# Order of the condition weights in the transfer queue of a two-block transformer kernel

## What is computed

```python
def first_block(x, p, ...):                      # 256 tokens, width 1024
    h = x
    for i in range(2):
        hn = rms_norm(h, g[0])
        y = mla_mixer(hn, ...) if i == 0 else dilated_mixer(hn, ...)
        h = h + rms_norm(y, g[1])                               # closing product w_o inside the mixer
        h = h + rms_norm(swiglu(rms_norm(h, g[2]), ffn_w_in[i], ffn_w_out[i]), g[3])
        h = h + (p[i] @ ple_w_proj[i]) * sigmoid(h @ ple_w_gate[i])
    return h

def second_block(x, c, ctx, c_ctx, w_ada, b_ada, ...):
    for l in range(2):
        sh1, sc1, gt1, sh2, sc2, gt2 = split(silu(c) @ w_ada[l] + b_ada[l], 6)      # w_ada[l]: 1024 x 6144
        csh1, csc1, ...              = split(silu(c_ctx) @ w_ada[l] + b_ada[l], 6)
        xn = modulate(rms_norm_2(h, ...), sh1, sc1); xc = modulate(rms_norm_2(hc, ...), csh1, csc1)
        ...   # attention, gating, neighbourhood attention with the bias na_rpb[l], then the experts
```

## Time and profile before

| what | us |
|---|---|
| median of 3 runs | 3183.58 |
| lowest, highest | 3181.65, 3187.3 |
| the profiled execution | 3185.1 |
| its span in the profile | 3183.4 |
| TensorE busy | 2817.2 (88%) |
| GpSimd busy | 1044.3 (33%) |

### The profile page before, as it was taken

How to read it: one execution, slowest core, us unless ns; L and a number is a source line. 1 busy time by engine, 2 the same in 40 slices (tenths; PEclk the granted TensorE clock), 3 DMA queues, 4 the chain that set the end, 5 groups by cost and what they waited for, 6 DMA issues and landing times. The chain is left out here.

```text
span 3183.4 us, 33959 instructions
## 1 busy us (share of the span) xinstructions
PE 2817.2 (88%) x13329; PEld 1876.5 (59%) x13329; DVE 1311.8 (41%) x2392; ACT 930.7 (29%) x1303; POOL 1044.3 (33%) x431
## 2 busy tenths in 40 slices
PE   7999959999998798799987999998597897999885
PEld 4777638887776486577875444443485775433331
DVE  5552123334523426763345333322527545332223
ACT  0433313335333313441212222222324332222211
POOL 0277528742875244043420000000363671000000
PEclk9999979999999899999988999999799998999998
DMA  5755675555556432222233999999242456999996
GB/s 179 265 181 177 246 280 177 181 169 179 182 186 237 161 103 81 81 92 75 100 119 142 383 421 422 422 422 402 106 137 75 146 206 273 411 422 422 422 422 266
DMA packets 208913, 746.03 MB, mean 234 GB/s; under 512 B 13877, under 2 KB 15075, under 8 KB 158833
## 3 DMA queue, kind: packets, MB, share of 16 engines
q1 hardware_dynamic: 189872, 669.61, 55.5%
q0 software_dynamic: 18880, 74.22, 6.8%
HBM read 721.00 MB, written 44.27 MB: 240 GB/s over the span
## 5 line engine op out<-in xcount | busy, mean ns | idle before, releaser
L1886 POOL TENSOR_TENSOR weight_ring_r<-weight_ring,weights_high_r 128x2048 fp32r<-128x2048 f32 x136 | 622.7, 4589 | 460.2 <-ACT weights_high_r L1495 370.0
L1495 ACT ACTIVATE weights_high_r<-weight_ring 128x2048 fp32r<-128x2048 f32 x136 | 257.1, 1901 | 654.2 <-PE banks L848 415.4
L843 PE MATMUL banks<-weights_high_r,x_transposed_r 128*128 128x512 f32 x1008 | 400.9, 398 | 32.6 <-DVE scaled_rows L2663 11.4
L2011 POOL DMA_DIRECT2D moe_y<-arena x64 | 34.1, 533 | 925.7 <-DVE arena L2711 925.7
L848 PE MATMUL banks<-weight_ring_r,x_transposed_r 128*128 128x512 f32 x1328 | 323.9, 390 | 1.0 <-POOL weight_ring_r L1886 1.0
L1886 POOL TENSOR_TENSOR weight_ring_r<-weight_ring,gates_r 128x2048 fp32r<-128x2048 f32 (+1 forms) x60 | 270.7, 4524 | 156.2 <-DVE small L2053 96.1
L848 PEld LDWEIGHTS banks<-weight_ring_r,x_transposed_r 128*128 128x128 f32 x1328 | 250.0, 188 | 53.4 <-POOL weight_ring_r L1886 1.4
L843 PEld LDWEIGHTS banks<-weights_high_r,x_transposed_r 128*128 128x128 f32 x1008 | 192.3, 191 | 77.4 <-issue 21.4
L1736 ACT ACTIVATE arena<-banks 64x1024 f32<-64x1024 f32 x64 | 65.1, 1018 | 488.8 <-PE banks L1237 488.8
L844 PE MATMUL banks<-weights_high_r,arena_r 128*128 128x512 f32 x520 | 206.7, 397 | 0.0
L2696 DVE TENSOR_TENSOR arena<-banks,arena 64x1024 f32<-64x1024 f32 x64 | 78.2, 1222 | 295.2 <-ACT arena L1736 295.2
(11 more groups left out here) (394 smaller groups left out, 4744.8 us busy)
## 6 DMA issues: line engine op xcount, KB each, us to landing
weight_ring<-in_moe_w_up SPq DMA_DIRECT2D x64, 1024.0 KB, 19.3
x_transposed<-in_moe_w_up SPq DMA_DIRECT2D x60, 1024.0 KB, 19.0
tokens_out<-in_moe_w_down SPq DMA_DIRECT2D x60, 1024.0 KB, 17.3
arena<-in_moe_w_gate SPq DMA_DIRECT2D x60, 1024.0 KB, 19.1
weight_ring<-in_moe_w_down SPq DMA_DIRECT2D x60, 1024.0 KB, 17.6
weight_ring<-in_w_in SPq DMA_DIRECT2D x56, 1024.0 KB, 5.2
weights_high<-in_moe_w_gate SPq DMA_DIRECT2D x56, 1024.0 KB, 18.7
weight_ring<-in_ffn_w_in SPq DMA_DIRECT2D x44, 1024.0 KB, 5.3
```

The costliest lines, as they stand in the source:

```text
L843: nc.tensor.matmul(banks[t][:, 0:width], xh, wh[:, k, :], start=k0 + k == 0, stop=False)
L1495: nc.scalar.activation(high(s, kn, width), slot(c, kn, width), ACT.Copy).then_inc(high_ready, 1)
L1886: nc.gpsimd.tensor_tensor(slot(c, kn, width, ring_r), slot(c, kn, width), high(s, kn, width), ALU.subtract).then_inc(low_ready, 1)
L2011: nc.gpsimd.dma_start(ys_dram[e * CAP:(e + 1) * CAP, :], A[own(e), E_Y:E_Y + D]).then_inc(ys_out[e % 2], 16)
```

## The change

The transfers are the same in number and size, and so are all products. What moves is when some of them are issued.

- The pieces `ff{i}` 0 to 2 were fetched in one go between the two chunks of the closing product. Now each is fetched by itself between groups of that product: behind group 4 of the first chunk, and behind groups 1 and 3 of the second.
- The pieces `dil` 0 and 1 are fetched ahead of the little projection of block 0 and `dil` 2 behind it, ahead of the first chunk of the dilated product. Before, 0 and 1 came behind the projection and 2 and 3 behind that chunk. The pieces 1 and 2 swap their spaces and with them what they wait for.
- At the end of block 1 the order was projection, `entry` pieces, context rows. It is now context rows, `entry` pieces, projection.
- GpSimd does the low parts of the first chunk of `g_ff_in[i]` before it issues the loads of a gain row and of `p`.
- GpSimd issues the repeated rows of the neighbourhood bias behind the last bias load of the dilated attention, instead of at the end of `close_block(0)`.

```diff
-            "dil": ([(left, right), (x_lo, x_hi), (low_a, low_b), (mid_a, h_hi)], (4608, 5120, 7680, 13824)),
+            "dil": ([(left, right), (low_a, low_b), (x_lo, x_hi), (mid_a, h_hi)], (4608, 5120, 7680, 13824)),
...
-        STREAM = []
+        STREAM, inside = [], {}
...
-            STREAM += chunks_of(g_ff_out[i])[:1] + [("fetch", ada[ff][0:3])] + chunks_of(g_ff_out[i])[1:] + [("ada", ff)]
-            STREAM += chunks_of(g_ple_g[i]) + [("fetch", ada[ff][3:])] + chunks_of(g_ple_p[i])
+            STREAM += chunks_of(g_ff_out[i]) + [("ada", ff)]
+            inside[g_ff_out[i], 0, 4] = ada[ff][0:1]
+            inside[g_ff_out[i], 1, 1] = ada[ff][1:2]
+            inside[g_ff_out[i], 1, 3] = ada[ff][2:3]
+            STREAM += chunks_of(g_ple_g[i]) + [("fetch", ada[ff][3:])]
             if closing is not None:
-                STREAM += [("fetch", ada["dil"][0:2]), ("ada", "dil")] + chunks_of(g_dil)[:1]
-                STREAM += [("fetch", ada["dil"][2:])] + chunks_of(g_dil)[1:] + chunks_of(g_dil_o)
-        STREAM += [("fetch", ada["entry"]), ("context", None), ("ada", "entry")]
+                STREAM += [("fetch", ada["dil"][0:2])] + chunks_of(g_ple_p[i])
+                STREAM += [("fetch", ada["dil"][2:3]), ("ada", "dil")] + chunks_of(g_dil)[:1]
+                STREAM += [("fetch", ada["dil"][3:])] + chunks_of(g_dil)[1:] + chunks_of(g_dil_o)
+            else:
+                STREAM += [("context", None), ("fetch", ada["entry"])] + chunks_of(g_ple_p[i]) + [("ada", "entry")]
...
                     freed.append((s, value))
+                    fetch(inside.get((g, n, i), []))
...
-                        sp.wait_ge(acc_ready, (ada_number[ada["ff0"][1]], end_of(g_ple_g[0]), ada_number[ada["ff0"][3]],
+                        sp.wait_ge(acc_ready, (ada_number[ada["ff0"][1]], ada_number[ada["ff0"][3]], end_of(g_ple_g[0]),
                                                ada_number[ada["ff0"][2]])[n])
...
             def close_block(i, g_o):
                 after_turn()
                 low_parts(g_o)
+                after_turn()
+                low_parts(g_ff_in[i], [0])
                 row(I["norm_g"][i, 3])
                 load(ar(PLE, 512).rearrange("p (k t) -> p k t", k=2), I["p_t"][i].rearrange("(k p) t -> p k t", p=P))
-                after_turn()
-                low_parts(g_ff_in[i])
+                low_parts(g_ff_in[i], range(1, D_FF // FF_PIECE))
                 low_parts(g_ff_out[i])
...
                 low_parts(g_ple_g[i])
-                if i == 0:
-                    nc.gpsimd.dma_start(rpb_skew.rearrange("r (q m) -> r q m", m=RPB_W),
-                                        rpb_dram.rearrange("l r w -> (l r) w").unsqueeze(1).broadcast_to(
-                                            [DEPTH * NA_H * RPB_R, GRID_W, RPB_W])).then_inc(rpb_out, 16)
...
             for j in range(2, N_PAIRS):
                 pool.wait_ge(dil_max, 4 * (j - 1))
                 load_bias(j)
+            nc.gpsimd.dma_start(rpb_skew.rearrange("r (q m) -> r q m", m=RPB_W),
+                                rpb_dram.rearrange("l r w -> (l r) w").unsqueeze(1).broadcast_to(
+                                    [DEPTH * NA_H * RPB_R, GRID_W, RPB_W])).then_inc(rpb_out, 16)
             close_block(1, g_dil_o)
```

## The result

| what | before | after |
|---|---|---|
| median, us | 3183.82 (3181.65 to 3187.3, 4 runs) | 3128.54 (3127.1 to 3132.13, 4 runs) |
| profiled execution, us | 3185.1 | 3127.39 |
| its span, us | 3183.4 | 3125.6 |
| TensorE busy | 2817.2 (88%) | 2811.8 (90%) |
| mean granted clock | 0.951 | 0.957 |

The ratio is 0.983, 95% interval 0.9816 to 0.9844: 55 us less on the medians, 57.7 us less between the two profiled executions. The forecast was 3117.0 with a range of 3108 to 3130, so the time lies in the range, 11.5 us over the point and 1.5 us under the upper end. Of the 66.9 us of the sum the two profiled executions show 57.7, a bit over eight tenths; what has to be explained are the missing 9 us.

The account below looks back on a forecast made before the run. TensorE, busy 88% of the span, was taken as the bound, so only its idle stretches could be won. 17.5 + 34.8 - 1.0 + 13.1 + 2.5 = 66.9 us off 3183.6 gave 3116.7, stated as 3117.0; range 3108 to 3130.

Parts of the forecast that it names:

- part C: Repeated rows issued behind the last bias load run into the burst at 757.69 us: about 1 us lost, bounds 0 and 8.
- Rival 1: Deliveries stay tight before the dilated product or at block 1's end, five to seven us late: about 3123 us, chance 0.10.
- rival 2: Spread pieces still drain the ring of weight slots in the closing product: 3134 us, half of it 3126; chance 0.07.
- Part A: Pieces spread through both blocks' closing products: no stall, 8.7 + 8.8 = 17.5 us won, bounds 0 and 11 named.
- 9.2 us of slack: Closing product, ring of four: a group is needed 16.3 us after issue; less 5.2 landing and 1.9 ScalarE leaves 9.2.
- Part B: Dilated pieces reordered and repeated rows gone between block 0 and the dilated product: VectorE's turn 34.8 us earlier, bounds 28 and 36.
- rival 4: Orders differ but waits don't; the long wait before the dilated product is the piece's own: 3183.6 us, chance 0.02.
- prediction's own sign: Prediction is wrong if a new transfer wait stands, most likely on dil 2 or a closing product group's high part.
- Part D: End of block 1: projection starts 10.3 us earlier and takes 2.8 us less, 13.1 us won, bounds 8 and 13.5.
- Part E: GpSimd's low parts ahead of its two loads in each block: 2 x 1.25 = 2.5 us won, bounds 0 and 4.
- rival 3: More than the sum: two lower-clock stretches in feed-forward first chunks go, turn at full clock: 3112 us, chance 0.05.
- Rival 5: Slower: repeated rows run into the burst at 757.69 us, costing 8 us at half share; over 3190 us, chance 0.02.

Follow-up runs that it names:

- two pieces at one place: Changed kernel with pieces ff 0 and 1 fetched together behind group 4 of the closing product's first chunk: 3127.83 us, ratio 0.9829.
- five-part kernel: Changed kernel with the repeated rows' copy cut into five transfers, each behind a bias load of the dilated attention: 3122.34 us (0.9809), again 3123.56 us (0.9813).
- undone run: Changed kernel with the old order at the end of block 1 (projection weights, entry pieces, context rows): 3140.93 us, ratio 0.9862.
- the early one: Changed kernel with the repeated rows issued behind the landing of the last ukv weights, at 62 us: 3128.05 us, ratio 0.9827.

## Why the prediction was right, and where it was 10 us off

The sum missed by 66.9 - 57.2 = 9.7 us, 6.5 of them in part C and 3.2 in the gate products. The time lies in the range, but not in the 3112 to 3122 that the forecast itself was given; the range reaches so far up because it also took in rivals 1 and 2 and the bound of part C. That the bound of part C was in it is no luck. That the gate products' 3.2 us, for which there was no row, still fitted in is.

**Part A** held as worked out, 8.7 and 8.8 us of second chunk. That the ring absorbs a piece at each place, against rival 2, is shown by the trace and by the two pieces at one place. It was tighter than the text had it: of the 9.2 us of slack 5.4 were to go for a piece and 3.8 to stay, and 2.5 stayed. What the step left out is a consequence behind the product: I had priced the lower clock inside the stall as gone for good, and 3.2 of its 6.5 us came back in the gate products. The forecast had no row for it.

**Part B** was 34.85 us against 34.8, its steps in the order of the text. That the 27.32 us came from the copy's company, against rival 4, was read rightly: with only the copy moved, 4.33 and 1.28 us of waiting are left. The two runs with only one half of the edit show that each alone would have left 8 to 13 us of the 34.9.

**Part C** is the step that failed, in its size and not in its mechanism. By the prediction's own sign, a new transfer wait, it failed plainly: ScalarE waits 10.76 us for the burst's first weights where it waited 2.10 before. I wrote "landing at 763 us, 5 us into the burst, which then runs some 4 us late", and "1 us lost". The length behind it was right: at 288 GB/s the copy's 7.86 MB take 27.3 us, with 4.7 us of issue ahead of them 32.0 us, and I had 31.3. The room of 2.6 us that I read from the earlier trace rows was right too. The term that was mis-sized is the lateness that those 5 us of overlap make: the burst's weights came 10.2 us late and not 4, and 10.2 less 2.6 is 7.6, the 7.5 us that the shift loses. (Without the copy the stretch at the lower clock would have cost 1.6 of them by itself; here it is hidden behind the late weights.) The 4 us were about the leftover's bytes alone (1.8 MB at the burst's 386 GB/s are 4.7 us). The leftover's bytes explain half of what was measured: at 727.9 us SyncE's queue had moved 2.1 MB, and the undisturbed burst of the five-part kernel had moved 4.1 MB as long after its start, so it is 2 MB or 5 us behind. The other 5 us are bytes of later transfers, moved ahead of their turn. When the first two halves have landed, at 732.43 us, the queue has moved 3.8 MB, 1.7 MB more than those two hold (0.3 MB in the five-part kernel at that point): it works on more transfers at once, and each ends later. When the second weights land it has moved 10.7 MB, where the kernel before had moved 8.7 MB by their landing: again 2 MB, or 5 us. That this follows from the copy's holding up the first ones is argued, not shown. The 7.5 us lie inside the bounds of 0 to 8 us that I gave, at the end that I had not taken.

The Trainium skill, page "DMA: Bandwidth & Descriptors", section "Anatomy of one DMA", would have made part C free; the trace speaks against it: 25.8 us after its issue the copy, alone until then at 288 GB/s, still had 1.8 of its 7.86 MB to move, and the five parts win 6 us. The Trainium skill's section "Issuing engines are not separate DMA queues" on the same page has all transfers interleave on the same engines; the trace agrees, and adds that the sharing was not even in the first 3 us, 0.91 MB to 0.00.

**Part D** gave 13.0 us against 13.1, and the undone run 11.9. **Part E** gave 2.5 against 2.5; the two stretches at the lower clock that rival 3 counted on going did go, but others came, so that rival is not what happened.

Rival 5, the slower one, named the right collision and priced it rightly at up to 8 us; to end slower than before it needed nine times that. Rival 1 came nearer in time than the forecast (3123) but at the wrong place: a delivery was late by more than five microseconds, but the deliveries before the dilated product and at the end of block 1 were not late.

**What stays open.** Why the gate product's first chunk drops to 1.2 GHz for 3.4 us once the closing product runs through isn't settled. The runs show that the stretch comes with the spread pieces and with none of the other edits, and that it stands behind a wait of 2.1 us for GpSimd that is equally long in both kernels; I tried nothing that changes this wait. The stretch at 732 us, which eight of the fourteen traces have, isn't explained either.

## What to carry to other kernels

A large background transfer has a cost wherever it overlaps a burst that the compute waits for, and moving it whole only moves the cost: find the stretches in which the queues stand empty, cut the transfer to their length, and put each part behind the small loads of its own queue, never ahead of them. Price what is left of it when the burst starts at more than its bytes: here 1.8 MB made a burst 10 us late, and the bytes were half of that. And when a stall is taken away, look for the first place behind it where TensorE still waits a little, since part of the clock that was won can be lost there.

## What the runs showed of the hardware

- The copy of 7680 KB from HBM to HBM by GpSimd's queue took 36.7 to 45.5 us as one piece (twelve traces, four places), its 9216 KB sister 35.2 to 39.1 us (fourteen). 4.7 us of the former are issue, in which none of its data flows; by itself it then moved at 288 GB/s, where SyncE's burst at the same place moved at 386. Its five parts took 8.1 to 10.9 us each, with 1.4 us of issue each.
- A small load behind such a copy on the same queue is held back with it: 28.6 us for 384 KB instead of 3.9. The sister copy behind the early one was issued only 0.5 us after that had landed.
- Beside such a copy, already under way, SyncE's queue moved nothing in a burst's first 3 us, where an undisturbed burst moved 0.5 MB, and the burst's first half landed after 14.0 us instead of 5.2. The issue of the six halves took 15.9 us of SyncE's time instead of 7.2.
- TensorE's granted clock in the gate product of block 0 went with an edit some 50 us upstream: the same matmuls behind the same 2.1 us wait ran at 2.4 GHz in the four traces with the stall in the closing product and partly at 1.2 GHz in the ten without.
